# The MLP's second products by one level of Strassen's scheme, with weight quarters summed in place by accumulating DMA transfers

## The reference

```python
D_FF = 4 * D_MODEL                     # 4096
        hm = rms_norm(x, g_mlp[l])
        x = x + jnp.square(jax.nn.relu(hm @ w_up[l])) @ w_down[l]
    return rms_norm(x, g_final)
```

## Time and profile before

| | |
|---|---|
| Median of 3 runs | 1576.82 us (1575.44 to 1581.01) |
| The profiled execution | 1579.46 us, its span 1577.7 us |
| PE busy | 1531.7 us (97% of the span) |
| DVE busy | 890.2 us (56%) |
| ACT busy | 715.3 us (45%) |
| POOL busy | 223.5 us (14%) |
| DMA | 141.56 MB, mean 90 GB/s; the core's queue q1 29.3% of 16 engines |

### The profile page before, as it was taken

One profiled execution on the slowest core, in us unless ns is written; L12 is line 12 of the kernel. 1 busy time (PEld: TensorE's weight loads), 2 busy tenths in 40 slices (PEclk: granted clock), 3 DMA queues, 4 the chain that ended last, 5 costly groups with the idle time before them and its releaser, 6 DMA issues.

```text
span 1577.7 us, 19176 instructions
## 1 busy us (share of the span) xinstructions
PE 1531.7 (97%) x7086; PEld 1239.6 (79%) x7086; DVE 890.2 (56%) x1753; ACT 715.3 (45%) x1630; POOL 223.5 (14%) x194
## 2 busy tenths in 40 slices
PE   7998999999999999999899999999999999999998
PEld 5886777877898777777587878788777888888886
DVE  6467485657565566666457557664455444434344
ACT  6553343334355667665335354442344433324243
POOL 3203020202120003122022005220001100000001
PEclk9999999999999999999999999999999999999999
DMA  6522121323424221112133312134323333333332
GB/s 194 161 68 80 54 80 55 107 68 120 119 76 147 77 61 56 54 56 67 41 121 94 94 55 67 56 109 131 93 81 94 94 93 96 105 94 93 97 103 81
DMA packets 88636, 141.56 MB, mean 90 GB/s; under 512 B 6368, under 2 KB 36448, under 8 KB 88544
## 3 DMA queue, kind: packets, MB, share of 16 engines
q1 hardware_dynamic: 87824, 139.55, 29.3%
q10 hardware_dynamic: 720, 0.80, 0.2%
HBM read 138.23 MB, written 2.10 MB: 89 GB/s over the span
## 4 chain that ended last, share of the span: by engine, by line
PE 79%; DVE 8%; ACT 5%; issue 3%; POOL 3%; DMA 2%; SPq 0%; ACTq 0%; POOLq 0%; DVEq 0%
PE banks L1259 12%; PE banks L1261 12%; PE banks L1260 12%; PE banks L1264 10%; PE banks L1266 10%; PE banks L1265 10%; PE banks L1222 3%; DVE sb_w_split L1964 3%; ACT sb_junk L1529 2%; DVE sb_arena L1973 2%; PE banks L1437 1%; PE banks L1384 1%; ACT sb_w_split L1561 1%; PE banks L1500 1%; DVE sb_arena L1964 1%
## 5 line engine op out<-in xcount | busy, mean ns | idle before, releaser
L1964 DVE TENSOR_TENSOR sb_w_split<-sb_raw,sb_w_split 128x512 fp32r<-128x512 f32 (+4 forms) x530 | 345.0, 693 | 365.9 <-ACT sb_w_split L1561 365.5
L1561 ACT ACTIVATE sb_w_split<-sb_raw 128x512 fp32r<-128x512 f32 (+4 forms) x530 | 288.1, 592 | 411.2 <-PE banks L1261 192.0
L1259 PE MATMUL banks<-sb_actA,sb_w_split 128*128 128x512 f32 x672 | 277.1, 412 | 2.8 <-DVE sb_arena L1964 2.5
L1261 PE MATMUL banks<-sb_actA,sb_w_split 128*128 128x512 f32 x672 | 263.0, 391 | 0.0
L1260 PE MATMUL banks<-sb_actA,sb_w_split 128*128 128x512 f32 x672 | 262.1, 390 | 0.0
L1264 PE MATMUL banks<-sb_w_split,sb_actB 128*128 128x512 f32 (+2 forms) x464 | 181.4, 391 | 1.6 <-DVE sb_w_split L1964 1.6
L1266 PE MATMUL banks<-sb_w_split,sb_actB 128*128 128x512 f32 (+2 forms) x464 | 175.9, 379 | 0.0
L1265 PE MATMUL banks<-sb_w_split,sb_actB 128*128 128x512 f32 (+2 forms) x464 | 175.5, 378 | 0.0
L1264 PE MATMUL banks<-sb_w_split,sb_actA 128*128 128x512 f32 (+1 forms) x384 | 154.4, 402 | 13.5 <-DVE sb_w_split L1964 9.6
L1259 PEld LDWEIGHTS banks<-sb_actA,sb_w_split 128*128 128x128 f32 x672 | 126.5, 188 | 32.7 <-issue 7.1
L1266 PE MATMUL banks<-sb_w_split,sb_actA 128*128 128x512 f32 (+1 forms) x384 | 150.3, 391 | 0.0
(11 more groups left out here) (226 smaller groups left out, 2188.2 us busy)
## 6 DMA issues: line engine op xcount, KB each, us to landing
sb_raw<-in_a_w_in SPq DMA_DIRECT2D x66, 256.0 KB, 3.0
sb_raw<-in_w_up SPq DMA_DIRECT2D x32, 512.0 KB, 3.8
sb_raw<-in_w_down SPq DMA_DIRECT2D x32, 512.0 KB, 3.8
sb_raw<-in_w_in SPq DMA_DIRECT2D x24, 512.0 KB, 3.7
sb_raw<-in_mem_w_kv SPq DMA_DIRECT2D x16, 512.0 KB, 3.8
sb_raw<-in_w_ckv SPq DMA_DIRECT2D x16, 512.0 KB, 3.8
sb_raw<-in_a_w_in SPq DMA_DIRECT2D x15, 512.0 KB, 3.7
sb_raw<-in_a_w_out SPq DMA_DIRECT2D x12, 512.0 KB, 3.9
```

The lines of the kernel that those rows point to most:

```text
L1259: pe.op.matmul(out, hi[:, cs], x.hi(k), start=i == 0, stop=False)
L1261: t = pe.op.matmul(out, lo[:, cs], x.hi(k), start=False, stop=last_i)
L1561: act.op.activation(hi[:, cs], raw[:, cs], ACT.Copy).then_inc(act.mark(m("w_hi"), 2 * n + part + 1), 1)
L1964: dve.op.tensor_tensor(out, a, b, op).then_inc(dve.mark(*mark) if mark else dve.tick(), 1)
```

## The change

Each block's second product, a 512 x 1024 activation F by a 1024 x 1024 weight W, is cut into quarters (256 tokens by 512 features; 512 features by 512 columns), and Strassen's scheme (in Winograd's arrangement) makes the four output quarters from seven products of quarters instead of eight. `dn{b}0/1` are replaced by `wn{b}0` to `wn{b}6`, in the order P1, P2, Q5, Q7, P6, Q3, N4. Each has two output tiles of 128 tokens by 512 columns, K = 512, two chunks and 24 matmuls.

- **Weights.** Four quarters of 1 MB are fetched whole by SP (`fetchR`) into four places, and POOL issues transfers that add another quarter from memory onto the one that lies there (`tsum`, `accum_op=ALU.add`, 512 KB each, eight for a block). Quarter 0 serves P1, then with quarter 1 added Q5, with quarter 3 added P6, and with quarter 2 added N4. Quarter 3 is added onto quarter 1 for Q7. A sum may be started when the former use of the place has been split, and its split waits for it. A chunk is split by one instruction of 1024 columns an engine, where there were two of 512.
- **Activations.** The squares stay in float32 (`f_plain`). DVE makes the first difference (`s1`), POOL three more (`ssum`, in two halves `hp` each). Every product's source is then rounded by ACT and subtracted by DVE (`g`: P1, P2, Q5, N4) or by POOL (`gp`: Q7, P6, Q3).
- **Outputs.** A `wn` tile is added to one or two places (`LANDS`): P1, Q5 and Q7 take two DVE instructions a tile, the others one. P1's and P6's common sum is kept in `first_sum`; for the other blocks it goes on, and after the last block POOL adds it in three steps `fix` of two instructions each.
- **Norm.** The norm factor is made as a row (`nrow`) and multiplied in when an `up` tile is evicted, instead of `r2` when a `dn` tile is.
- **Order.** `up{b}g` takes its weights in two parts of 256 columns. `wn` products take two of eight PSUM banks each in turn. The last block's Q3 and N4 carry `fsq`, `fin` and `store` of tokens 0, 1 and 2, 3.

```diff
+P1, Q5, P6, P2, Q7, Q3, N4 = range(7)
+WINO_ORDER = (P1, P2, Q5, Q7, P6, Q3, N4)
+WEIGHT = {P1: 0, Q5: 0, P6: 0, N4: 0, Q7: 1, P2: 2, Q3: 3}
+ADDED = {Q5: 1, P6: 3, Q7: 3, N4: 2}
+LANDS = {P1: (("x", 0, 0, ALU.add), ("sum", 0, 0, ALU.subtract)), P2: (("x", 0, 0, ALU.add),),
+         Q5: (("x", 0, 1, ALU.add), ("x", 1, 1, ALU.add)), P6: (("sum", 0, 0, ALU.add),), Q3: (("x", 0, 1, ALU.add),),
+         Q7: (("x", 1, 1, ALU.add), ("x", 1, 0, ALU.subtract)), N4: (("x", 1, 0, ALU.subtract),)}
...
-            add(f"up{b}{g}", ("w_up",), D_MODEL, [(b * D_MODEL + g * 512, 512)], "feature", "hE", "relu")
-        for half in range(2):
-            add(f"dn{b}{half}", ("w_down",), D_MODEL, [(half * 512, 512)], "token", f"f{b}", "tok", k0=b * D_MODEL)
+            add(f"up{b}{g}", ("w_up",), D_MODEL, [(b * D_MODEL + g * 256 + c, 256) for c in (0, 512)], "feature", "hE", "relu")
+        for i in range(7):
+            add(f"wn{b}{i}", None, 512, [(0, 512)], "token", f"F{b}{i}", "wn" if len(LANDS[i]) == 1 else "wn2",
+                tokens=SEQ // 2)
...
-    p.side(0, [("sqp", "e", 7)], lag=0)
-    p.side(0, (), ("nsq", "e"), ("esum",), lag=4000)
+    scales(0, "e", after=[("sqp", "e", 7)])
     for j in range(TT):
         for g in range(2):
             p.side(0, (), ("xt", j, g))
+    for i in (0, 1):
+        p.put(("fetchR", 0, i))
+    for i in (3, 2):
+        p.side(0, (), ("fetchR", 0, i))
+    for c in range(2):
+        p.side(0, (), ("tsum", 0, Q7, c), lag=0)
...
     for b in range(4):
-        for g in range(2):
-            p.product(f"up{b}{g}", [("esum",)], lambda j: [(("relu", b, 4 * g + j),)])
-        last = b == 3
-        p.product(f"dn{b}0", [("xt", TT - 1, 1)], (lambda j: [(("fsq", 0, j), ("fg", j))]) if last else None)
-        p.product(f"dn{b}1", tail=(lambda j: [("fsq", 1, j), ("fin", j), ("store", j)]) if last else None)
+        if b:
+            p.soon.extend([[("fetchR", b, i)] for i in (1, 0, 2, 3)] + [[("tsum", b, Q7, 0)], [("tsum", b, Q7, 1)]])
+        p.product(f"up{b}0", [("nrow", "e")], into=banks(4) if b else (0, 1, 2, 3),
+                  tail=lambda j: [("relu", b, up_tile(0, j))])
+        p.soon.extend([[("g", b, P1, 0)], [("g", b, P2, 0)], [("s1", b, 0), ("g", b, Q5, 0)], [("ssum", b, 3, 0)],
+                       [("gp", b, Q7, 0)], [("ssum", b, 2, 0)], [("gp", b, P6, 0)], [("ssum", b, 4, 0)]])
+        p.product(f"up{b}1", into=banks(4) if b else (0, 1, 2, 3),
+                  tail=lambda j: [("relu", b, up_tile(1, j))] + ([("g", b, P1, 1)] if j == 1 else []))
+        if b == 0:
+            p.need(("tsum", 0, Q7, 1))
+        work = {P1: [[("g", b, P2, 1), ("tsum", b, Q5, 0)], [("s1", b, 1), ("g", b, Q5, 1)], [("tsum", b, Q5, 1)], [("ssum", b, 3, 1)]],
+                P2: [[("gp", b, Q7, 1), ("tsum", b, P6, 0)], [("ssum", b, 2, 1)], [("gp", b, P6, 1), ("tsum", b, P6, 1)],
+                     [("ssum", b, 4, 1)]],
+                Q5: [[("gp", b, Q3, 0)], [("gp", b, Q3, 1)]], Q7: [[("g", b, N4, 0)], [("g", b, N4, 1)]],
+                P6: [[("tsum", b, N4, 0)], [("tsum", b, N4, 1)]], Q3: [], N4: []}
+        if b == 3:
+            work[Q3] = [[("fix", 0)], [("fix", 1)], [("fix", 2)],
+                        [(kind, *([1] if kind == "fsq" else []), j) for j in (2, 3) for kind in ("fsq", "fg")]]
+        for i in WINO_ORDER:
+            p.soon.extend(work[i])
...
+            p.product(f"wn{b}{i}", into=banks(2), tail=tail, whole=b == 3 and i == N4)
...
+                if i in ADDED:
+                    act.wait_ge(m(f"dma_sum{i}{c}"), 16 * (b + 1))
+                else:
+                    act.wait_ge(m(f"dma_quarter{WEIGHT[i]}"), 16 * (b + 1))
+                act.wait_ge(*m.chunk_done(n - SPLIT_SLOTS))
+                act.op.activation(hi, raw, ACT.Copy).then_inc(act.mark(m("w_hi"), 2 * n + 2), 2)
+                continue
...
-                scalar(v.relu[:, 4 * int(name[-1]) + j, :], src, 0.0, ALU.max, empty, place.after)
+                dve.wait_ge(*m.emptied(("nrow", "e")))
+                fused(v.relu[:, j % 2, :], src, 0.0, ALU.max, v.row["e"], ALU.mult, empty, place.after)
...
+        elif kind == "tsum":
+            b, i, c = a
+            if i == Q7:
+                pool.wait_ge(m("dma_quarter1"), 16 * (b + 1))
+            else:
+                pool.wait_ge(*m.wino_split(b, {Q5: P1, P6: Q5, N4: P6}[i], c))
+            r0, c0 = b * D_MODEL + 512 * (ADDED[i] // 2) + 256 * c, 512 * (ADDED[i] % 2)
+            pool.op.dma_start(v.wino_weight(i, c), v.io["w_down"][r0:r0 + 256, c0:c0 + 512].rearrange("(k p) n -> p k n", p=P),
+                              accum_op=ALU.add).then_inc(m(f"dma_sum{i}{c}"), 16)
...
+        elif kind == "fix":
+            n = a[0]
+            for u in range(2):
+                pool.wait_ge(*m.evicted(f"wn3{P6}", u))
+                pool.wait_ge(*m.evicted(f"wn3{Q7 if n else Q5}", u))
+                x = (v.x_tok[:, u, 512:], v.x_tok[:, 2 + u, 512:], v.x_tok[:, 2 + u, 0:512])[n]
+                tensor(x, x, v.first_sum[:, u, :], ALU.subtract if n == 2 else ALU.add, *(m.at("fixed", step) if u else ()))
...
+            if b == 0 and i >= 2:
+                sp.wait_ge(*m.emptied(("xt", TT - 1, 1)))
+                sp.wait_ge(*m.at("t_lo", ("turn", "hE", KD - 1)))
+                sp.wait_ge(*m.at("sq", ("sqa", "e", KD - 1)))
```

More of the change, by code:

```diff
@@ L269, in source_step @@
         return ("cval", k // 2)
-    if src[0] == "f":
-        return ("relu", int(src[1]), k)
+    if src[0] == "F":
+        b, i = int(src[1]), int(src[2])
+        return ("gp" if i in (P6, Q3, Q7) else "g", b, i, k // 2)
     return ("turn", src, k)
@@ L408, in need, with product @@
                 self.force(step)
-    def product(self, name, before_ev=(), soon=None, into=None, first=True, tail=None):
+    def product(self, name, before_ev=(), soon=None, into=None, first=True, tail=None, whole=False):
         pr = PRODUCTS[name]
@@ L415, in product @@
         ks, i, n_j = k_tiles(name), 0, n_out(name)
-        spans = [(c,) for c in range(len(pr.order))] if tail is None else [(0,), tuple(range(1, len(pr.order)))]
+        spans = [tuple(range(len(pr.order)))] if whole else [(c,) for c in range(len(pr.order))]
         for span in spans:
@@ new lines, in order_of_work, with banks @@
+    for c in range(2):
+        p.side(0, (), ("tsum", 0, Q7, c), lag=0)
+    bank = 4
+    def banks(n):
+        nonlocal bank
+        bank = (bank + n) % 8
+        return [(bank - n + i) % 8 for i in range(n)]
+    for b in range(4):
+        if b:
[18 more added lines that the diff above has]
+            p.soon.extend(work[i])
+            tail = None
+            if b == 3 and i == P2:
+                tail = lambda j: [("fsq", 0, j), ("fg", j)]
+            elif b == 3 and i in (Q3, N4):
+                tail = lambda j: [(kind, *([int(i == Q3)] if kind == "fsq" else []), 2 * (i == N4) + j)
+                                  for kind in ("fsq", "fin", "store")]
+            p.product(f"wn{b}{i}", into=banks(2), tail=tail, whole=b == 3 and i == N4)
@@ L997, in __init__ @@
         at = Layout(self.arena)
-        self.out_sb = at.take(TT, D_MODEL)
-        self.relu, self.sq = at.take(KD, SEQ), at.take(2, SEQ)
+        at.at = 4096
+        flat = self.x_res[:, :, :].rearrange("p a b -> p (a b)")
+        first = Layout(self.arena).take(2, 4 * 512)
+        self.w_quarter = [w.rearrange("p (k n) -> p k n", k=4) for w in
+                          (first[:, 0, :], first[:, 1, :], flat[:, 0:2048], flat[:, 2048:4096])]
+        self.f_plain, self.relu = at.take(KD, SEQ), at.take(2, SEQ)
         at.at = 9280
         self.x_tok, self.g_row = at.take(TT, D_MODEL), at.take(D_MODEL)
+        self.out_tile = [a[:, i, :] for a in (flat[:, 0:2048].rearrange("p (a b) -> p a b", a=2),
+                                              first[:, 1, :].rearrange("p (a b) -> p a b", a=2)) for i in range(2)]
+        self.first_sum = at.take(2, 512)
+        at.at = 19520
+        self.s_plain = at.take(2, 512)
+        self.row["e"] = at.take(SEQ)
         def squares_at(ring, total, n=2):
@@ L1174, in raw_total, with wino_split @@
     def raw_total(self, n):
-        return 16 * sum(len(PRODUCTS[self.plan.chunks[m][0]].parts) for m in range(n % RAW_SLOTS, n + 1, RAW_SLOTS))
+        return 16 * sum(len(PRODUCTS[self.plan.chunks[m][0]].parts) for m in range(n % RAW_SLOTS, n + 1, RAW_SLOTS)
+                        if not is_wino(self.plan.chunks[m][0]))
+    def wino_split(self, b, i, c):
+        return self("w_lo"), 2 * self.plan.chunk_of[f"wn{b}{i}", c] + 2
 class Stream:
@@ L1611, in scalar_program @@
             j = a[0]
-            half = v.out_sb[:, j, 0:512]
+            early = 512 * (j // 2)
+            half = v.out_tile[j][:, early:early + 512]
             act.wait_ge(*m.at("f_g", ("fg", j)))
@@ L1936, in evict_waits @@
         return [m.at("rot", ("rot", "k", TT - 1))]
-    if kind == "up" and name[-2] != "0":
```

(9 more changed lines are left out.)

165 lines of the change are left out of this document (132 added, 33 removed).

## The result

| | before | after |
|---|---|---|
| Median | 1576.13 us (1574.98 to 1581.01, 4 runs) | 1620.87 us (1619.06 to 1623.53, 4 runs) |
| Span of the profiled execution | 1577.7 us | 1621.7 us |

The ratio is 1.0279, 95% interval 1.0252 to 1.0306. The likeliest direction was right. The size was not: 44.7 us by the medians instead of 5 us, past the upper end of 1607.

What follows compares the result with a forecast made beforehand. PE's matmul count was taken to bound the MLP. From 1579.5 us: -21.8 matmuls, +15.2 stops, 0 sums, +3.5 first block, +0.5 `nrow`, +7.5 end gave 1584.4, or 1582 for a median; range 1563 to 1607.

Steps and rivals of the forecast that it cites:

- The likeliest direction: Whole kernel: slower, above 1585 us, chance 0.45.
- L: Time of an accumulating transfer from issue to landing, taken as 6 us; allowed up to 8.7, 7.0 or 8.6 by place.
- rival 2: Sums come late, L of 9 to 13 us, at P6's second half: 1592 to 1612 us, centre 1600; chance 0.28.
- the costs at 10 and 12 us: Late sums: L of 10 us costs 4.4 us a block, 18 in all; L of 12 costs 30.
- the part on traffic: Weight fetches: 8 MB a block for `w_down` instead of 4, hidden from the second block on at 302 GB/s.
- The end: Last matmul to DVE's last `fin`: four chains, 11.0 us instead of 3.3, costing 7.5; bounds 3 and 9.5.
- First block: Quarters 3 and 2 start late, quarter 2 arriving 2.9 us late for ACT; cost taken as 3.5, bounds 0 and 8.
- sums: no cost: Accumulating transfers: at L of 6 us every sum lands before its split wants it, so 0 us.
- the same walk: Step-by-step timing of the diff's order from P1's start, checking when each split and sum is done against when wanted.
- the term of 1.5 us a block for POOL: Seven products: POOL's contention costs DVE 3.6 us, perhaps half of it where no lead is left; 1.5 a block.
- the 2.3 us for P2's second and Q5's first chunk: PE waits for late splits: 1.1 us at P2's second chunk and 1.2 at Q5's first, each block.
- 6.5 us a block at full contention: Upper bound of PE's stops, with full contention and a further wait on ACT: 26 us; 15.2 was taken.

Runs made afterwards that it cites:

- ring1408: The changed kernel with the room for descriptors of POOL's transfers raised from 1024 to 1408 bytes: 1598.8 us, ratio 1.0147.
- plain_load: The changed kernel, room 1024, with POOL's 32 transfers overwriting instead of adding (output not the reference's): 1595.1 us, ratio 1.0115.
- gq5_late: The changed kernel with room 1408 and s1 and g of Q5's second half put behind the split of P2's second chunk: 1597.7 us, ratio 1.0153.

## Why the prediction was wrong

- **The direction, the matmuls, the price of a sum, the end.** PE's matmuls went as said, 96 fewer in the second products. L is 5.8 us, taken as 6, and in time against the thresholds of 7.0 us and more: rival 2, as it was put, did not happen. The 6 was an estimate ("twice the data") that no run shows, and so were the costs at 10 and 12 us, which no run had to pay: beside the seven products of after no add took over 6.2 us, and q0 lists the same 16.78 MB for adds as for plain transfers, but 8704 packets instead of 4608 and 6.4% of the 16 engines' span instead of 3.3%. The 302 GB/s of the part on traffic are 139.55 MB in 29.3% of 1577.7 us. The end cost 6.8 us, 7.5 predicted, by the four chains in DVE's queue that the prediction named; POOL's `fix`, which the prediction put in front of them, was over at 1606.45, 2.1 us ahead of PE's end. First block: the wait for quarter 2 was 1.6 us on ACT and 0.87 on PE, 3.5 predicted; the 14.1 us to land of the page is a median over all blocks, most of them not waited for.
- **The step that failed first** is "sums: no cost" in the part on accumulating transfers. Each sum was held against its own threshold with L alone. That a second one could not be issued until the first had landed was nowhere in it, since the trace of before has no transfer from POOL and I took the issue for free at any rate. In its place the runs show one add under way at a time, 4.7 to 5.0 us of POOL's wait ahead of a second one, and 22 us gained by more room: more than half of the miss. With room for two the same walk holds.
- **The second is the term of 1.5 us a block for POOL.** From the earlier trace rows I made a rate, 0.65 us lost for each us of POOL, times the share of DVE's time. The rows allow another reading: the instruction of 1.78 us ended 0.55 us after POOL's, so what counts is where POOL stands when the DVE instruction starts. A run of POOL behind the issue of a transfer held a single split for up to five instructions, and it did so where ACT's half had just come late, not on average. In a steady block with room, the stops are 4.6 to 5.2 us; 1.8 remain without POOL's work. So the 2.3 us for P2's second and Q5's first chunk were near, 1.8, and the 1.5 for POOL were 2.8 to 3.4 there, and more in blocks 0 and 3. The bound that the prediction named, 6.5 us a block at full contention, was set aside for the mean.
- **Missing altogether** was what stops of PE do to its clock (below), 5.7 us.
- Added up from the two profiled executions, which are 44.0 us apart in span where the sum had 4.9, a miss of 39.1: stops 46.9 instead of 15.2 + 3.5, so 28.2; half clock 5.7; the end 0.7 less; and the 6.4 not itemised instead of 0.5 for `nrow`, 5.9. By the experiments the room is worth 22 of it and POOL's sums 17, of which 6 were in the sum, so 11, each with the half clock behind its stops; the other 6 us no run separates.
- **The signs named** held for P2 and Q5 (1.38 and 1.64 us in block 1 of after, 1.1 and 1.2 said), for DVE (34.2 us busy in the seven products of block 1, over 34 said), and for the wait of ACT on a transfer, which was to prove rival 2: it came, but through the room. The direction was not luck, though the largest cost was missed: with that cost gone ring1408 is still 1.5% slower than before.

What this leaves for the scheme: with POOL's sums nearly free it still stood at 1582.9, since 12.3 us of stops and 8.6 more at the end (11.9 instead of 3.3) eat 20.9 of the 21.8 that the matmuls give, and some 5 us in gaps too short to be counted come on top. Whether an order with the four end chains laid side by side and POOL's work in small portions would beat before was not tried.

## What to carry to other kernels

Before moving transfers to POOL's queue, look at how many can be under way with the room of the build: here one add of 272 packets with 1024 bytes and two with 1408, and the second was worth 22 us. Where DVE and POOL both read SBUF, price a meeting by what POOL is at when the DVE instruction starts, not by a mean share. Of the 16 splits of 1.21 us that were held in the MLP stage of after, 15 were held for one POOL instruction and took up to 2.8 us, and one for five (7.61 us; 7.09 in ring1408), in a run that stood right behind the issue of a transfer. Do not queue long runs there if a split is due. A chain of evict, square, mean, root and scale should not stand in one engine's queue in front of the next tile's eviction: four of them cost 6.8 us here.

## What the hardware showed that I had not expected

- An accumulating transfer of 512 KB landed in 5.8 us and kept POOL for 1.2 (after), a plain one in 4.4 and 0.73 (plain_load); 272 packets against 144.
- After stops PE went on at half clock. The first three stretches are of after, the last of ring1408 (us, PE, PEld, DVE, ACT, POOL, clock, DMA share, GB/s):

```profile
1292.00:1296.00 4.00, 4.00 (x10) 3.13 (x11) 0.94 (x1) 1.06 (x1) 2.77 (x3) 0.50 0.36 65
...
1584.00:1586.00 2.00, 2.00 (x6) 1.52 (x6) 2.00 (x4) 0.00 (x0) 0.00 (x0) 0.50 0.00 0
...
1588.00:1592.00 4.00, 4.00 (x19) 3.30 (x18) 3.75 (x7) 1.90 (x2) 1.21 (x1) 1.00 0.35 47
...
1378.00:1381.00 3.00, 3.00 (x8) 2.31 (x7) 3.00 (x6) 0.09 (x1) 0.79 (x1) 0.50 0.00 0
```

PE is busy throughout in all four, yet has 10 matmuls in 4 us at a granted clock of 0.50 and 19 at 1.00. Starts are 0.43 us apart instead of 0.227. In block 0 of after it lasted from 1291.8 to 1296.7, behind the stop of 10.2 us, and came again from 1307.4 to 1310.8, behind one of 3.0; in block 3 from 1583.6 to about 1587, behind one of 8.0. That is 4 and 1.7 us lost. Behind stops of 3 us in blocks 1 and 2 of after nothing of it was seen, yet in ring1408 a stop of 2.2 us in block 1 was followed by 0.50 from 1377.7 to 1381.1, and every other kernel with room 1408 shows the like in block 1 or 2. So the length of one stop does not tell whether it comes, and a forecast has to leave room for it: it is how gq5_late lost again what its shorter stops had given.
